# Attention rounds issued in twos: both transposes, then both scores, then the projections, then the weighing

## The reference, cut to what matters

```
q  = rmsnorm(c_q)  @ w_q_b     # (S, 8, 96): 64 plain + 32 rotary
kv = rmsnorm(c_kv) @ w_kv_b    # (S, 8, 128): 64 key, 64 value
s  = q_nope . k_nope + q_rope . k_rope
p  = softmax(s * 96**-0.5)     # over 512 keys
attn = p @ v
pool = multiscale_pool(u)
x  = x + concat(attn, pool) @ w_out
```

## Time and profile before

| | us |
|---|---|
| median of 3 runs | 1148.1 (1147.04 to 1148.65) |
| the profiled execution's own time | 1144.88 |
| its span | 1143.1 |
| PE busy in the span | 1117.8 (98%) |
| attention, first turn to the end of the second weighing half of pair 3 | 130.55 to 273.07 on the span's clock |

### The profile page before, as it was taken

How to read it: one execution, slowest core, us unless ns; L and a number is a source line. 1 busy time by engine, 2 the same in 40 slices (tenths; PEclk the granted TensorE clock), 3 DMA queues, 4 the chain that set the end, 5 groups by cost and what they waited for, 6 DMA issues and landing times.

```text
span 1143.1 us, 15837 instructions
## 1 busy us (share of the span) xinstructions
PE 1117.8 (98%) x5146; PEld 896.6 (78%) x5146; DVE 826.1 (72%) x1170; ACT 555.4 (49%) x986; POOL 464.2 (41%) x405
## 2 busy tenths in 40 slices
PE   8999999999999989999999999999999999999996
PEld 7787766665888867888888888888888888888885
DVE  7784976674468899878787878787876757757555
ACT  6312687775223454545454545454554545533332
POOL 0185642322566046765676567655310202211000
PEclk9999999999999999999999999999999999999999
DMA  6610000104652126444544454445896565533341
GB/s 209 222 44 26 1 12 13 38 19 164 204 202 104 56 81 205 165 138 152 178 165 138 154 176 165 138 155 172 330 344 204 190 197 192 168 108 118 92 143 74
DMA packets 138431, 161.60 MB, mean 141 GB/s; under 512 B 8755, under 2 KB 105354, under 8 KB 133770
## 3 DMA queue, kind: packets, MB, share of 16 engines
q1 hardware_dynamic: 138080, 160.82, 42.0%
q10 hardware_dynamic: 298, 0.11, 0.0%
HBM read 115.55 MB, written 45.35 MB: 141 GB/s over the span
## 4 chain that ended last, share of the span: by engine, by line
PE 86%; DVE 10%; issue 2%; ACT 1%; POOL 1%; DMA 0%; DVEq 0%; SPq 0%; POOLq 0%; ACTq 0%
PE ps L298 26%; PE ps L299 26%; PE ps L300 26%; PE ps L869 2%; PE ps L850 2%; DVE WL L2050 1%; PE ps L711 1%; PE ps L861 1%; DVE XL L1727 1%; DVE SF L2149 1%; DVE SF L2157 1%; DVE WDHL L1907 1%; DVE col L1918 1%; DVE XT L1721 0%; DVE R L1900 0%
## 5 line engine op out<-in xcount | busy, mean ns | idle before, releaser
L298 PE MATMUL ps<-XH,WH 128*128 128x512 f32 x722 | 287.1, 398 | 0.8 <-DVE WL L339 0.5
L300 PE MATMUL ps<-XH,WL 128*128 128x512 f32 x722 | 281.2, 390 | 0.0
L299 PE MATMUL ps<-XL,WH 128*128 128x512 f32 x722 | 281.1, 389 | 0.0
L298 PEld LDWEIGHTS ps<-XH,WH 128*128 128x128 f32 x722 | 135.6, 188 | 32.4 <-issue 3.0
L299 PEld LDWEIGHTS ps<-XL,WH 128*128 128x128 f32 x722 | 135.7, 188 | 29.1 <-issue 2.2
L300 PEld LDWEIGHTS ps<-XH,WL 128*128 128x128 f32 x722 | 135.5, 188 | 28.5
L298 PE MATMUL ps<-GHL,WH 128*128 128x512 f32 x394 | 153.6, 390 | 0.8 <-DVE WL L2050 0.7
L300 PE MATMUL ps<-GHL,WL 128*128 128x512 f32 x394 | 153.3, 389 | 0.0
L299 PE MATMUL ps<-GHL,WH 128*128 128x512 f32 x394 | 153.3, 389 | 0.0
L334 ACT ACTIVATE WH<-WR 128x1024 fp32r<-128x1024 f32 (+3 forms) x45 | 45.5, 1011 | 138.7 <-PE ps L300 129.4
L1476 ACT ACTIVATE SF<-ps,col 128x512 f32<-128x512 f32 x88 | 68.2, 778 | 74.6 <-PE ps L300 65.6
(11 more groups left out here) (241 smaller groups left out, 2250.8 us busy)
## 6 DMA issues: line engine op xcount, KB each, us to landing
TL<-in_w_up SPq DMA_DIRECT2D x48, 256.0 KB, 3.6
s_scratch<-XT SPq DMA_DIRECT2D x11, 1024.0 KB, 4.7
XT<-in_w_down SPq DMA_DIRECT2D x11, 1024.0 KB, 6.5
t_scratch<-XT SPq DMA_DIRECT2D x11, 1024.0 KB, 3.8
WR<-t_scratch SPq DMA_DIRECT2D x44, 256.0 KB, 2.7
TL<-s_scratch SPq DMA_DIRECT2D x44, 256.0 KB, 2.9
WR<-in_w_up SPq DMA_DIRECT2D x40, 256.0 KB, 3.5
WR<-in_w_down SPq DMA_DIRECT2D x33, 256.0 KB, 3.7
```

The lines of the kernel that those rows point to most:

```text
L298: pe.matmul(out, wh, xh, start=first, stop=False, skip_group_check=skip)
L299: pe.matmul(out, wh, xl, start=False, stop=False, skip_group_check=skip)
L300: return pe.matmul(out, wl, xh, start=False, stop=last, skip_group_check=skip)
```

## The change

Only the order of PE's instructions changes. The rounds are taken by two: for even u, turn u and turn u+1 stand together, then scores u+3 and u+4, then the projections and mixes of both rounds (`beside`), then the weighing of both (`weighing`). The instructions, their waits and the orders of ACT, DVE, POOL and SP are the same. The two new functions hold the old conditions word for word.

```diff
+            def beside(i, u, last):
...
+            def weighing(i, u):
+
+                if i == 0:
+                    if u == 12:
+                        weigh(0, 0, (0, 1))
+                else:
+                    if u == 3:
+                        weigh(i - 1, 1, (0, 1))
+                    if u == 6:
+                        weigh(i - 1, 1, (2, 3))
+                    if u == 10:
+                        weigh(i, 0, (0, 1))
+                if u == 14:
+                    weigh(i, 0, (2, 3))
+
             def pair(i, last):
-                for u in range(4 * TT):
+                for u in range(0, 4 * TT, 2):
                     turn(i, u)
-                    if u + 3 < 4 * TT:
-                        scores(i, u + 3)
-                    elif not last:
-                        scores(i + 1, u + 3 - 4 * TT)
...
+                    turn(i, u + 1)
+                    for v in (u + 3, u + 4):
+                        if v < 4 * TT:
+                            scores(i, v)
+                        elif not last:
+                            scores(i + 1, v - 4 * TT)
+                    for v in (u, u + 1):
+                        beside(i, v, last)
+                    for v in (u, u + 1):
+                        weighing(i, v)
```

More of the change, by code:

```diff
@@ L872, in weigh @@
                     ins.then_inc(o_ready, 1)
+            def beside(i, u, last):
+                if i == 0:
+                    if u == 0:
+                        pe.wait_ge(c_lo, 6)
+                        project_q(0, 2, qf_ready, 2)
+                    if u == 2:
+                        project_q(0, 3, qf_ready, 3)
+                    if u == 4:
+                        pe.wait_ge(k_lo, 4)
+                        mix(6)
+                    if u == 5:
+                        mix(7)
+                    if u == 6:
+                        project_q(1, 0, qf_ready, 4)
+                    if u == 8:
+                        project_k(1, 0, qf_ready, 5)
+                    if u == 9:
+                        pe.wait_ge(mix_lo, 2)
+                        values(1, 0)
+                else:
+                    if u == 0:
+                        values(i, 1)
+                    if u == 1:
+                        project_q(i, 3, k_lo, i * 4 + 4)
+                    if u == 5 and not last:
+                        project_q(i + 1, 0, qf_ready, i * 4 + 4)
+                    if u == 7 and not last:
+                        project_k(i + 1, 0, qf_ready, i * 4 + 5)
+                    if u == 8 and not last:
+                        values(i + 1, 0)
+                if not last:
+                    if u == 11:
+                        project_q(i + 1, 1, k_lo, i * 4 + 6)
+                    if u == 13:
+                        project_q(i + 1, 2, qf_ready, i * 4 + 6)
+                    if u == 15:
+                        project_k(i + 1, 1, qf_ready, i * 4 + 7)
```

## The result

The changed kernel took 1162.6 us in the median of four executions (1160.1 to 1163.5) against 1147.8 of the kernel before, a ratio of 1.0129 (95% interval 1.0114 to 1.0144). In a second comparison it was 1161.9 against 1147.0, 1.0119 (1.0098 to 1.0140). It is slower by 14 to 15 us. The forecast was 1159.8 with a range of 1153 to 1166.

What follows compares the result with a forecast made beforehand. PE was taken to bound attention, so its new waits of 3.8 + 1.8 + 1.85 + 1.7 + 2.5 = 11.65 us, with no saving, add to the median 1148.1 and give 1159.8 us. The range was 1153 to 1166.

Steps and rivals of the forecast that it cites:

- saving of adjacent turns: PE in attention: a turn followed by a turn saves 0, with 30 x 0.09 = 2.7 us as far bound.
- turn 11, pairs 1 and 2, each: Turn 11 waits for exponent 11, behind scale_rows, k_split and k_low: 1.89 us, twice, 3.8 us.
- project_q(i, 3), pairs 1 to 3, each: At the pair's start it waits for k_low, 0.8 to 1.0 against 0.30 before: three times 0.6 us.
- pairs 1 and 2 in all, each: The stretch from turn 0 of pair 1 to that of pair 2 should grow by about 2.5 us.
- pair 3 in all: All new waits of pair 3: project_q(3, 3), turn 7 and its later turns, 4.2 us.
- pair 0: New waits at turns 1, 4, 5, 7, 9, 11, 13: 5.5 less idle of about 3, 2.5 us (0 to 4).
- sum of the waits: All new waits of PE in attention added over the four pairs: 11.65 us.
- clock (rival 1): The clock falls in the new gaps, 1.6 us each, up to 4.8 on top: 1164.6; chance 0.14.
- The reading of the bound: In attention PE is the bound, busy 30.36 of 30.5 us; its waits go one to one into the end.
- turn 7: In pair 3 it waits for exponent 7, behind a weights split twice as wide: 1.85 us, no less than 1.5.
- Rival 2: scale_rows holds DVE less long and pair 0 absorbs its waits: 5.9 us in all, 1154; chance 0.14.
- Rival 3: The 0.09 us step is a switch and the waits are covered: 2.7 us go, 1145.4; chance 0.07.

Runs made afterwards that it cites:

- e10_fill_again: Changed kernel with six filler matmuls in each of three gaps, measured again beside the unaltered changed kernel: 1158.0 us against 1161.9.
- e7_middle_twos: Changed kernel with pairs 0 and 3 round by round, pairs 1 and 2 in twos with k_split, values copy, k_low and scale_rows moved later: 1147.5 us, ratio 1.0000.
- e2_late_k: Changed kernel with the next pair's k_split and values copies on ACT and k_low on DVE moved from round 8 to round 9: 1156.1 us.
- e3_fill: Changed kernel with six filler matmuls between turns 10 and 11 of pairs 1 and 2 and turns 6 and 7 of pair 3: 1158.5 us.

## Why the prediction was right

By its own steps, with the pure waits taken from stretches in which the clock stayed at 1.00 (the profile after for pairs 0 and 2, e10_fill_again for pair 3):

| term | forecast | measured |
|---|---|---|
| saving of adjacent turns | 0 | 0 (0.87 us for eight transposes; e7_middle_twos) |
| turn 11, pairs 1 and 2, each | 1.9 | 1.7 (196.38 less 194.21 and 0.44) |
| project_q(i, 3), pairs 1 to 3, each | 0.6 | 0.4 (38.38 of e2_late_k less 37.95) |
| pairs 1 and 2 in all, each | 2.5 | 2.05 |
| pair 3 in all | 4.2 | 3.9 (37.6 less 33.7) |
| pair 0 | 2.5 | 3.1 |
| sum of the waits | 11.65 | 11.1 |
| clock (rival 1) | 0 | 3.2 in the profile after |

The reading of the bound held: PE was the bound, and every us of new wait went into the time. That the whole effect lay in attention, and that it was not given back, held as well.

The wait at **turn 11** was sized 0.16 too long, since DVE was free 0.08 earlier, exponent 10 stood 0.67 and not 0.72 behind its maximum, and turn 11 0.83 and not 0.85 behind its exponential. **project_q(i, 3)** began 4.26 us after the pair's first turn (212.77 to 217.03 in pair 2), where the chain of the prediction had 4.4 to 4.6: k_low started at 2.80, 0.61 behind k_split, and did not have to wait for maximum 3. In **pair 3** turn 7 stood 2.30 us behind turn 6 (265.88 to 268.18), so 1.86 late, against 1.85 forecast. **Pair 0**, the least certain term, had four long waits (0.78, 0.98, 1.01 and 1.20 idle at turns 1, 4, 5 and 7), as followed, and one at the values that was not foreseen (0.67 idle, on mix_low); those at turns 9, 11 and 13 did not come. The prediction took 5.5 less about 3 that the pair idled anyway. PE idles 4.75 us there now (40.30 less 35.55 busy), and it had idled 1.64 before (37.23 less 35.59): both numbers were too high, and that the term came out near is partly luck.

What the forecast left out is the **clock**. It was the first rival, priced at 1.6 us a fall, and given 0.14. It was not an alternative to the forecast but came on top of it, in part: two falls in the attention of the profiled execution (3.2 us), and falls in three of the four pairs of the next profile. Why the step failed: I compared one idle of 2.13 us that a fall followed with one of 1.7 that none followed, and read a border between them. The runs show no such border. The falls came behind six of thirteen idles of 1.55 to 1.70 us, and in pair 0 behind idles of 0.78 and of about 1.0; and behind the idle of 2.13 us itself, 2.15 in the changed kernel's profile, the clock stayed (last section). e3_fill and e10_fill_again point to the idle in the gaps as the cause: with the gaps filled, the clock in pairs 1 to 3 is 1.00 in both profiles. So the clock, put at nothing, is the term that was wrong, and it is most of what is missing; the median stayed inside the range because that reached up to rival (1). With the measured 11.1 + 3.2 and the 0.9 outside attention the span's 15.2 are complete. 1159.8 + 2 to 3 for the clock would have been 1162 to 1163.

The page that was weighed, the Trainium skill's TensorE: Matmul & The Clock Gate, Part 4: PE-mode transpose, says that transposes do not count as busy for the clock as matmuls do. The falls here stand where two turns in a row meet a gap, which agrees with it, but twos of turns without a gap brought no fall (clock 1.00 in both pairs of e7_middle_twos), and the runs do not separate the transposes from the idle, since no kernel had such a gap among matmuls alone in attention. That stays open.

**Rival 2** (the waits come out at half) fell with every run. **Rival 3** (a saving of 2.7 us) fell with e7_middle_twos, as the run of sixteen transposes in the earlier trace rows had said. (The prediction counts thirty places; four pairs with eight each make 32, which changes nothing.)

## What to carry to other kernels

When an engine that sets the end has its instructions regrouped, ask for each wait what used to stand between the producer's start and this wait, and then look at what is queued ahead of the producer on the other engines, whose orders were written for the old sequence. A start-to-start pitch that is long behind one kind of instruction may belong to the instruction before it; a long run of that kind tells. A wait on TensorE can cost more than its length, because matmuls behind it may run at the lower clock, so price a new gap like these (0.8 to 1.7 us idle) with a fall of the clock in part of the executions.

## What the runs showed of the hardware

The clock's falls cost what they slow: in pair 1 of the profile after, the stretch with the gap of 1.56 us idle, and the one behind it:

```profile
194.00:196.30 2.30, 0.83 (x8) 0.59 (x7) 2.24 (x5) 1.83 (x5) 0.48 (x2) 1.00 0.00 0
196.30:199.70 3.40, 3.32 (x10) 2.83 (x11) 1.80 (x3) 2.41 (x7) 0.00 (x0) 0.53 0.00 0
```

Matmuls of 512 columns stood 0.43 us apart there, the 1.2 GHz level, in place of 0.23 (the chain of waits, behind the gap and ahead of it):

```profile
197.87 0.43 PE ps L299
...
186.96 0.23 PE ps L299
```

One fall made pair 1, 2 or 3 1.6 us longer. At the same gap of pair 2, with the same 1.56 us idle, the clock stayed in this execution and fell in the next. The fall that the kernel before had on its way into the feed-forward cost it nothing. Its stretch, and below it the wait ahead of the same 35 us of the changed kernel and these themselves, 14.56 later, where the clock did not fall though PE had stood idle as long:

```profile
415.00:450.00 35.00, 33.55 (x139) 26.63 (x139) 34.54 (x43) 20.38 (x33) 25.06 (x18) 0.96 0.49 164
...
428.89 0.50 PE L298 MATMUL ps<-CHL,WH 128*128 128x512 f32 x1 [2.15 <-DVE WL L2063]
...
429.56:464.56 35.00, 32.29 (x139) 25.42 (x138) 34.54 (x43) 20.34 (x33) 25.05 (x18) 1.00 0.49 164
```

Both hold 139 matmuls, and DVE is busy 34.5 of the 35 us: it sets the pace there.

Filler matmuls in a wait, into a bank that is overwritten, are worth 3 to 4 us here where three waits are left, and cost nothing while they end before the wait does (40.0 us a pair with them and without, at a clock of 1.00).
